# Two-model block kernel, matrix-memory layer: tile rounding and splits in halves over blocks, output-gate units cut in two, gate transposes between value units

## The reference

```
q, k, v, o, gates = split(u @ w_in)            # q,k 8x64, v 8x128, o 1024, gates 4x8
b = cumsum(log_f);  d = b[t] - b[s] + log_i[s]  # lower triangle
m_t = max(max_s d, b + m0)
wq = exp(d - m_t) * (q @ k.T)
num = wq @ v + exp(b + m0 - m_t) * (q @ C0)
h = num / max(|sum wq + ...|, exp(-m_t))        # forward and, flipped, backward
hn = (hf + hb) * rsqrt(mean((hf + hb)^2) + eps) * head_norm
y = (hn * sigmoid(o)) @ w_out
```

## Time and profile before

| what | value |
|---|---|
| median of 3 runs | 2445.49 us (2441.13 to 2446.42) |
| the profiled execution | 2443.79 us |
| span of its profile | 2442.0 us |
| mean granted TensorE clock | 0.96 of 2.4 GHz |
| TensorE busy | 2269.7 us |
| VectorE busy | 1679.6 us |
| ScalarE busy | 885.2 us |
| GpSimd busy | 672.5 us |

### The profile page before, as it was taken

The page is one execution under the profiler, slowest core; times in us unless marked ns, Lnnn a source line. Parts: engine busy times, 40 slices in busy tenths (PEclk is TensorE's granted clock), DMA queues, the critical chain, the costliest instruction groups (busy, mean ns, idle before and its releaser), DMA issues. The chain is left out here.

```text
span 2442.0 us, 31167 instructions
## 1 busy us (share of the span) xinstructions
PE 2269.7 (93%) x12408; PEld 1892.2 (77%) x12408; DVE 1679.6 (69%) x2431; ACT 885.2 (36%) x1357; POOL 672.5 (28%) x434
## 2 busy tenths in 40 slices
PE   5999999899999889999988888878999998898998
PEld 5887678688888678899987666656888887657997
DVE  6665658988669955767777845569876775596343
ACT  1323333222333233444433445542223334244444
POOL 3001210233345500113465022212323462002244
PEclk9999999999999989999988989889999999899999
DMA  8422124455555462356655421113655564203652
GB/s 278 153 87 74 47 87 155 138 198 181 189 190 185 141 188 77 114 162 192 216 173 161 146 82 61 52 52 132 212 179 201 190 172 97 69 1 106 189 173 86
DMA packets 268025, 341.14 MB, mean 140 GB/s; under 512 B 31056, under 2 KB 181464, under 8 KB 267624
## 3 DMA queue, kind: packets, MB, share of 16 engines
q1 hardware_dynamic: 266704, 334.92, 42.8%
q10 hardware_dynamic: 1176, 4.23, 0.5%
HBM read 338.04 MB, written 1.08 MB: 139 GB/s over the span
## 5 line engine op out<-in xcount | busy, mean ns | idle before, releaser
L646 PE MATMUL PS<-a_h,w_h 128*128 128x512 f32 (+1 forms) x2808 | 974.9, 347 | 43.8 <-DVE a_l L1689 28.5
L647 PE MATMUL PS<-a_l,w_h 128*128 128x512 f32 (+1 forms) x2808 | 961.8, 343 | 0.0
L648 PE MATMUL PS<-a_h,w_l 128*128 128x512 f32 (+1 forms) x2808 | 961.3, 342 | 0.0
L1509 DVE TENSOR_TENSOR w_l<-ring,w_h 128x1024 fp32r<-128x1024 f32 (+1 forms) x434 | 596.9, 1416 | 257.0 <-ACT w_h L1145 256.3
L646 PEld LDWEIGHTS PS<-a_h,w_h 128*128 128x128 f32 x2808 | 541.2, 193 | 138.0 <-issue 57.4
L1145 ACT ACTIVATE w_h<-ring 128x1024 fp32r<-128x1024 f32 (+1 forms) x434 | 426.7, 1033 | 583.1 <-PE PS L648 529.5
L648 PEld LDWEIGHTS PS<-a_h,w_l 128*128 128x128 f32 x2808 | 540.9, 193 | 59.6
L647 PEld LDWEIGHTS PS<-a_l,w_h 128*128 128x128 f32 x2808 | 541.8, 193 | 56.0
L1530 DVE SCALAR_TENSOR_TENSOR bias<-ring,silu,bias 128x512 f32<-128x512 f32 x532 | 453.3, 906 | 4.2 <-DMA ring<-in_w_mod 0.5
L2076 POOL TENSOR_TENSOR a_l<-hid,a_h 128x2048 fp32r<-128x2048 f32 (+1 forms) x60 | 228.4, 3807 | 241.6 <-ACT a_h L1161 241.6
L2091 POOL TENSOR_TENSOR hid<-hid 128x256 f32<-128x256 f32 (+1 forms) x128 | 157.7, 1233 | 414.8 <-ACT hid L1127 414.8
(11 more groups left out here) (181 smaller groups left out, 2379.6 us busy)
## 6 DMA issues: line engine op xcount, KB each, us to landing
ring<-in_w_ff SPq DMA_DIRECT2D x64, 1024.0 KB, 5.7
ring<-in_ffn_w SPq DMA_DIRECT2D x64, 1024.0 KB, 5.5
ring<-in_w_mod SPq DMA_DIRECT2D x48, 1024.0 KB, 5.2
ring<-in_ada_w SPq DMA_DIRECT2D x48, 1024.0 KB, 5.2
ring<-in_w_in SPq DMA_DIRECT2D x42, 1024.0 KB, 5.3
ring<-in_mlstm_w_in SPq DMA_DIRECT2D x12, 1024.0 KB, 5.6
ring<-in_w_o SPq DMA_DIRECT2D x8, 1024.0 KB, 5.0
ring<-in_w_attn_out SPq DMA_DIRECT2D x4, 1024.0 KB, 5.6
```

The lines of the kernel that those rows point to most:

```text
L646: nc.tensor.matmul(out, stat[0], mov[0], start=start, stop=False, **kw)
L647: nc.tensor.matmul(out, stat[0], mov[1], start=False, stop=False, **kw)
L648: return nc.tensor.matmul(out, stat[1], mov[0], start=False, stop=stop, **kw)
L1509: V.tensor_tensor(w_l[:, n % 2, c], ring[:, split_raw[n] % SLOTS, c], w_h[:, n % 2, c].bitcast(F32), ALU.subtract).then_inc(s_wl, 1)
```

## The change

Six edits, none to what is computed:

1. The phase `m_gates` goes. Its transposes go to PSUM bank 5, after the second of the four value units of `m_in`; VectorE copies the columns there, without a wait between the four copies. A semaphore `m_gate_columns_ready` tells GpSimd and VectorE.
2. `dense_slots` becomes `piece(b)`: 28 pieces in 28 of 32 blocks (none in 8, 17, 26, 31). A piece is half an output-gate unit (four of eight k) or a whole value unit.
3. `round_w` and `split_w` in the loop become halves: the tile after next is rounded in the first and second block after the end of a tile, split in the second and third, behind L2010. `TILE_ENDS` ends with tile 5, so the loop prepares tiles 1 to 7; tile 8 is left to `to_h`.
4. On ScalarE head output, exponential, rounding of the output and logarithm are in other blocks and all before `turned`; on VectorE the exponent goes to a head's first block, `normed` and `rest_out` behind L2010.
5. The mean square of a head comes one block earlier, its square too.
6. The last head's mean square moves into the first tile of `to_h`, whose two units are now interleaved over k: k 0 to 5 of both, the mean square, k 6 and 7.

```diff
-            phase("m_gates", units=1, **base)
...
-        def dense_slots(ph):
-
-            units = [(i, j) for i, st in enumerate(ph["steps"]) for j in range(st["units"])]
-            return {3 * k // 2: unit for k, unit in enumerate(units)}
...
+        def piece(b):
+
+            p = b - (b // 9)
+            return (p // 4, p % 4) if b % 9 < 8 and p < 28 else None
+
+        TILE_ENDS = {-1: -1, 0: 3, 1: 7, 2: 12, 3: 16, 4: 21, 5: 25}
+
+        def tile_to_prepare(b, since):
+
+            return next((i + 2 for i, end in TILE_ENDS.items() if end + since == b), None)
...
+                        if ph["src"] == "m" and i == 0:
+                            for ks in (range(0, 6), range(6, 8)):
+                                if ks[0]:
+                                    mean_square(MH - 1)
+                                for k in ks:
+                                    if k == KC // 2:
+                                        second_half(st)
+                                    pe.wait_ge(s_xl, ph["x"] - KC + k + 1)
+                                    for c in range(2):
...
+                            mod_unit(st)
+                            continue
...
                             if i == 5:
                                 tokm(st, u + j, w, j)
+                                if j == 1:
+                                    gate_columns()
...
-                            tokm(st, st["u"] + j, w, j)
+                            tokm(st, st["u"] + q, w, q)
                         else:
-                            fm(st, st["u"] + j, w, slice(P * j, P * j + P), from_a, ALL)
+                            j, half = divmod(q, 2)
+                            uu = st["u"] + j
+                            out = PS[:, bank_of[uu], :] if half else bank(uu)
+                            if half:
+                                second_half(st)
+                            for k in range(4 * half, 4 * half + 4):
+                                mm = product(out, [view8(x)[:, k, P * j:P * j + P] for x in w], from_a(k), k == 0, k == 7)
+                            if half:
+                                mm.then_inc(s_unit, 1)
...
-                        if b % 4 == 3 and b > 4:
+                        if b % 4 == 2 and b > 4:
                             mean_square(b // 4 - 1)
                     values(2 * MH - 1)
-                    mean_square(MH - 1)
...
                     for b in range(n):
-                        if b % 4 == 0 and b >= 8:
-                            log_variance(b // 4 - 2)
+                        hh, qt = b // 4, b % 4
                         scale(b)
                         if b + 2 < n:
                             decay(b + 2)
...
+                        if qt == 1 and hh >= 1:
+                            head_out(hh - 1)
+                        if qt == 1 and hh >= 2:
+                            norm_and_gate(hh - 2)
+                        for i in range(2):
+                            t = tile_to_prepare(b, 1 + i)
+                            if t is not None:
+                                round_half(ph["s"] + t, i)
+                        if qt == 3 and hh >= 1:
+                            log_variance(hh - 1)
+                        if qt == 3 and hh >= 2:
+                            round_out(hh - 2)
+                        if piece(b) is not None and piece(b)[0] % 2 == 0 and piece(b)[1] % 2:
+                            output_gate(piece(b)[0], piece(b)[1] // 2)
                         turned(b)
-                        if last_of_tile(ph, b):
-                            round_w(ph["steps"][slots[b][0]]["s"] + 2)
-                        if b % 4 == 0 and b >= 12:
-                            round_out(b // 4 - 3)
...
-                        if last_of_tile(ph, b - 1):
-                            split_w(ph["steps"][slots[b - 1][0]]["s"] + 2)
...
                         dve.wait_ge(s_scaled, b + 1)
                         V.scalar_tensor_tensor(out=x0, in0=x1, scalar=rc[:, 1:2], in1=x0, op0=ALU.mult, op1=ALU.add
                                                ).then_inc(s_P, 1)
+                        for i in range(2):
+                            t = tile_to_prepare(b, 2 + i)
+                            if t is not None:
+                                split_half(ph["s"] + t, i)
+                        if qt == 2 and hh >= 2:
+                            normed(hh - 2)
+                        if qt == 0 and hh >= 3:
+                            rest_out(hh - 3)
```

More of the change, by code:

```diff
@@ L1067, in values @@
                         mm.then_inc(s_mpv, 1)
[L1069 to L1073 removed]
                     def dense(b):
[L1077 removed]
+                        if piece(b) is None:
                             return
[L1079 removed]
+                        i, q = piece(b)
                         st = ph["steps"][i]
@@ L1939, in scan_rows, with gate_columns @@
                             step(ins)
+                    def gate_columns():
+                        dve.wait_ge(s_cols, 1)
+                        src = PS[:, 5, :].rearrange("p (w t g n) -> p w t g n", w=2, t=4, g=2, n=32)
+                        for what in range(2):
+                            for d in range(2):
+                                ins = V.tensor_scalar(tm[:, what, :, :, d], src[:, what, :, d, 0:MH],
+                                                      -1.0 if what == 0 else 1.0, None, ALU.mult)
+                        ins.then_inc(s_tm, 1)
                     for i, st, u in steps_of(ph):
@@ L1948, in _ @@
                             copy_unit(u + j, mv[:, j, 0:256], slice(0, 256))
-                elif kind == "m_gates":
-                    wait_units(dve, u)
-                    dve.wait_ge(s_unit, u + 1)
-                    src = PS[:, bank_of[u], :].rearrange("p (w t g n) -> p w t g n", w=2, t=4, g=2, n=32)
-                    for what in range(2):
-                        for d in range(2):
-                            ins = V.tensor_scalar(tm[:, what, :, :, d], src[:, what, :, d, 0:MH],
-                                                  -1.0 if what == 0 else 1.0, None, ALU.mult)
-                            if not (what and d):
-                                step(ins)
-                    ins.then_inc(s_free[bank_of[u]], 1)
+                            if j == 1:
+                                gate_columns()
                 elif kind == "m_heads":
@@ L1997, in _ @@
                         V.reciprocal(rc, rc).then_inc(s_rc, 1)
-                        if b - 1 in slots and slots[b - 1][0] % 2:
-                            i, j = slots[b - 1]
-                            copy_unit(ph["steps"][i]["u"] + j, mv[:, j, 128 * i + 128:128 * i + 384], slice(0, 256))
-                        if last_of_tile(ph, b - 1):
-                            split_w(ph["steps"][slots[b - 1][0]]["s"] + 2)
-                        if qt == 1 and b >= 12:
-                            rest_out(hh - 3)
-                        if qt == 1 and b >= 8:
-                            exponent(hh - 2)
-                        if qt == 3 and b >= 8:
-                            normed(hh - 2)
+                        if qt == 0 and hh >= 2:
+                            exponent(hh - 2)
+                        before = piece(b - 1) if b else None
+                        if before is not None and before[0] % 2:
+                            i, j = before
+                            copy_unit(ph["steps"][i]["u"] + j, mv[:, j, 128 * i + 128:128 * i + 384], slice(0, 256))
                         dve.wait_ge(s_scaled, b + 1)
@@ L2177, in _ @@
                             args(b + 2)
[L2178 removed]
+                        if b % 4 == 1 and b >= 4:
                             square_out(b // 4 - 1)
```

78 lines of the change are left out of this document (40 added, 38 removed).

## The result

The changed kernel takes 2401.91 us (median of 4 runs, 2399.51 to 2402.80) against 2443.86 us before (4 runs, 2441.13 to 2446.42): a ratio of 0.9827, 95% interval 0.981 to 0.9844, so 1.7% faster and clear of the noise. The forecast was 2406, the range 2393 to 2430.

What follows compares the result with a forecast made beforehand. The prediction took the stage to be bound by latency, TensorE's transposes waiting for VectorE's last combination. Stage -48.6 us and tail +9.5 gave -39.1, so 2404.7, forecast as 2406 against the median; range 2393 to 2430.

Steps and rivals of the forecast that it cites:

- Pieces and halves: Stage: pieces outlast the 2.0 to 2.3 us chain in 28 filled blocks; tile halves mostly fit in slack.
- the sum: Stage: 146.9 us work plus idling 9.5, less 0.5 for the start, plus 3.5 clock loss: 159.4 against 208.0.
- the 5 us allowed: Blocks 8, 17, 26 and 31, without a piece: 1.3 us of idling each, 5 us together.
- the 1 us for halves that meet other work: Two of 32 blocks: VectorE's work with a split half needs 5.4 us against 5.0; 1 us taken.
- the 3 us for GpSimd: Stage: GpSimd's argument addition can hold VectorE, between nothing and 33 us; 3 us taken.
- The clock: Stage: a fall or two behind the empty blocks, 3.5 us lost, half of 7 us at the lower level.
- The rival in which the clock stays as before: Stage still spends 61 us at 1.2 GHz, losing 25.6 instead of 3.5: 2428; chance 0.13.
- The beginning: Stage start: first query-key product moves from 1418.7 to about 1418.2; the 3.57 us weighting wait falls to about 0.5.
- Work: Stage: TensorE's work at full clock 146.9 us; eight more pipeline fills, under 1 us.
- The tail: Output projection: TensorE waits of 2.9 and 4.6 us, VectorE ends 7.7 later; +9.5 us in all.
- The 1.8 added for the clock: Output projection: two close gaps of 2.9 and 4.6 make the clock fall once, partly hidden under VectorE.
- the tail is free: Behind the stage: VectorE makes up its delay before the norm, only the stage counts: 2396.5; chance 0.10.

Runs made afterwards that it cites:

- all tiles whole: Changed kernel with the loop's tiles rounded and split whole again, as in the kernel before: 2423.50 us, 0.9918 of before.
- all gates whole: Changed kernel with each output-gate unit as 24 products in its second block, none in its first: 2421.33 us, 0.9909 of before.
- the pieces alone: Kernel before with only the 28 pieces in 28 of 32 blocks, tiles still prepared whole: 2426.60 us, 0.9935 of before.
- the second profile: Profile of the unaltered changed kernel, run again beside the tail experiments: 2401.93 us, 0.9828 of before.
- gates alone: Kernel before with only the gate transposes moved between two value units: 2439.54 us, 0.9988 of before.
- halves alone: Kernel before with only tile preparation in halves, tile 8 still in the loop, dense units whole: 2420.31 us, 0.9912 of before.
- the run with both edits: Changed kernel with tile 8 prepared right behind the loop and the last mean square after k 0 to 2: 2392.96 and 2394.30 us in two groups.

## Why the prediction was right

The forecast of 2406 was 4 us too high, less than 0.2%. By its steps, with the profile after:

- **Pieces and halves.** It held that the waits of the transposes for the last combination would disappear in filled blocks. They did: 2.6 us are left, all in blocks without a piece. Idling of the stage is 5.0 us, where the sum had 9.5. The four empty blocks took 4.0 of the 5 us allowed: 1.32, 0.59 and 0.70 for the transposes, and 1.35 in block 31, where most of it comes from the order on ScalarE and not from the missing piece. Of the 1 us for halves that meet other work one wait of 0.30 for a weighting is left (block 9, behind a split half), and the 3 us for GpSimd were not needed.
- **What the sum did not say** is how the gain divides. It treated pieces as the cure and knew the halves only as a cost of 1 us. Alone the pieces gain 15.5 us and the halves 21.8; taking either back from the change (all tiles whole, all gates whole) costs 19 to 22 us. In the expectation for the pieces alone the term "about 1.5 us each" for seven blocks was mis-sized: it held for the three blocks with a value unit (1.5 to 2.1), but the four without a piece cost 3.0 to 4.6.
- **The clock.** Predicted 3.5 us lost, measured 3.3 (6.50 us busy in one stretch of 6.83, halved) and none in the second profile; the agreement with 3.5 is partly luck. The rival in which the clock stays as before is out: 0.98 and 1.00 against 0.85. Its argument was not empty, though: in the kernel with gates whole the clock fell five times, behind or in waits of 1.3 to 2.2 us.
- **The beginning.** The wait for the first weighting went from 3.57 to 0.69 us, where 0.5 was expected. The stage began at 1416.46 rather than 1418.2 in this execution, but at 1422.05 in the second, so this says nothing of the change.
- **Work.** 149.1 us at full clock against 146.9. The sum named "under 1" for the pipeline fills of the eight cut units and then left it out. The rest is probably the estimate by halving the busy time at half clock. Over stages without cut units it gives 146.9 with 61.4 us at half clock (before), 147.3 with 51.2 (gates alone) and 148.3 with 30.7 (halves alone), so it comes out low where much time is at half clock.
- **The tail.** Predicted waits 2.9 and 4.6, measured 2.96 and 4.25. VectorE's last square came 7.4 us later behind the values, where 7.7 was worked out, and the end of the projection 7.2 later. The 1.8 added for the clock was too much: it fell (3.4 us from 1592.88), but on VectorE, which ends last, little of it shows. In the second profile it fell for 10.24 us from 1591.26; TensorE's end came 8.5 later and VectorE's square 7.7. That the rival "the tail is free" is wrong is shown by the run with both edits, 7.6 us faster.

So the mechanism was right, and the closeness of the number is in part errors that cancel: idling 4.5 and the tail 2.3 too high, the work 2.2 too low.

## What to carry to other kernels

When engines work in turn on short blocks, measure the bare chain of a block once (here 2.0 us), and ask of every block whether the engine that is to stay busy has that much independent work, and whether a long operation of another engine stands in the chain; both must hold, and each cured alone gave 15.5 and 21.8 of the 42 us. After moving work out of a loop's last pass, look at who prepares the first step behind the loop: here two moves of a few lines behind it were worth another 7.6 us. An idle microsecond on TensorE was worth more than one: in the kernel before 35 us of idling came with 26 us lost at half clock.

## What was not expected of the hardware

- Falls of TensorE's clock behind waits as short as 1.3 to 1.9 us (gates whole; with halves alone three falls came behind waits of 1.55, 1.73 and 1.87), where I had taken from the kernel before that it takes gaps of 3 us and more. Its profile had such gaps at falls (the earlier trace rows is one, of 4.08) and a stretch of 20.5 us with 0.6 us of idling at 1.00; for gaps between those two sizes it did not decide.
- The same program had one stretch of 6.83 us at half clock in one profile of the stage and none in the next; the gaps of its first 3 us (0.52 and 0.69) were the same in both. Differences of 3 us between two profiles of this kernel can be that alone.
